# The pre norm's factor behind the FFN products: scaled on the gate, left to the post norm on the linear half

## The chip, the cores and the metric

The kernel runs on one core of one Trainium2 chip. Its metric is the time of one execution on the device in microseconds. Before the change it took 1862.63 us (median of 3 runs, 1861.44 to 1865.62).

The engines are TensorE (PE in the profile; PEld is its weight load), VectorE (DVE), ScalarE (ACT), GpSimd (POOL) and SyncE (SP), which issues the DMAs. Each engine works through its own list of instructions in the order in which it is written, and waits on semaphores.

## The reference, cut to what matters

Two transformer blocks on 272 tokens (16 meta tokens and 256 real ones) of width 1024. The first block is FFN 1, a mixer with two kinds of attention, and FFN 2. The second has a convolution, a third attention and 32 experts. The change is in the two FFNs of the first block:

```python
def rmsnorm(x, g):
    xf = x.astype(jnp.float32)
    y = xf * lax.rsqrt(jnp.mean(xf * xf, axis=-1, keepdims=True) + EPS)
    return (y * g.astype(jnp.float32)).astype(x.dtype)

def swiglu(h, w_gate, w_up, w_down):
    return (jax.nn.silu(h @ w_gate) * (h @ w_up)) @ w_down
...
        f = swiglu(rmsnorm(h, ffn1_pre_g[l]), ffn1_w_gate[l], ffn1_w_up[l], ffn1_w_down[l])
        h = h + 0.5 * rmsnorm(f, ffn1_post_g[l])
        m = hybrid_mixer(rmsnorm(h, mix_pre_g[l]), ...)
        h = h + rmsnorm(m, mix_post_g[l])
        f = swiglu(rmsnorm(h, ffn2_pre_g[l]), ffn2_w_gate[l], ffn2_w_up[l], ffn2_w_down[l])
        h = h + 0.5 * rmsnorm(f, ffn2_post_g[l])
```

Let r be the pre norm's factor of a token, rsqrt(mean + EPS). The gate product of the normed input is r times that of h times g, and so is the up product. Silu needs the factor. The up half is linear in it, and the post norm divides any factor of a token out again, but for its EPS, which has to be scaled along.

## The kernel before, in words

Tokens lie along the free dimension: 272 columns in FFN 1, 256 in FFN 2 (the meta tokens are left out there). The 1024 features are 8 tiles of 128 partitions (k = 0 to 7), and the 2816 hidden features are 22 tiles (j = 0 to 21). Every float32 product of the dense part is made of three (L676 to L678): input and weights are each split into a high part in the format fp32r and the rest, a low part.

**Weights.** They come as a stream of pieces of 128x2048 (1 MB) through a ring of 6 slots. SP issues piece p when the semaphore freed has reached p+1. ACT copies a piece into w_hi (split_piece, L1356; the copy is L1363). DVE subtracts it from the piece into w_lo (rest, L1803; L1806). There are three pairs of buffers, and ACT may overwrite one when PE has begun the piece behind its last user. An up tile j takes one piece: 8 blocks for the gate and 8 for the up half, 48 products in all.

**An FFN.** PE works through 22 up tiles into banks 2(j%2) and 2(j%2)+1, and then through 8 down tiles of 22x3 products (11 more pieces). Tile j waits for w_lo of its piece and for the hidden product of tile j-2, which frees the banks. Per tile ACT does: high part of piece j+2, Silu of the gate bank into sig (L1389). DVE does: w_lo of piece j+2, the product sig x up bank (L1886), the copy to hid_hi (L1889), the difference hid_lo (L1891), and one ada reduction (L1874; 48 tiles of another matrix, 33 in FFN 1 of which 22 lie in its up tiles, 15 in the first up tiles of FFN 2). The down products ask for hid_lo of tile k one after another.

**Ahead of an FFN.** ACT squares the residual (L1346), PE sums over partitions with a matrix of ones (L657), ACT takes the root as Ln and Exp (L1353, L1354), DVE multiplies by gain and factor into x_all (L1786), ACT copies to x_hi (L1369), DVE subtracts to x_lo (L1842). Only then does the first product of that k start. In FFN 2 the residual of the mixer (L1786, L1829) lies ahead of all this. Dummy products (L672) fill PE meanwhile.

**Behind the dense part.** SP waits for the last dense pieces and products and then loads 32 experts of 12 MB each, one behind the other (L606); each of their slots is refilled once the one ahead has been used.

## Time and profile before

| | |
|---|---|
| median of 3 runs | 1862.63 us (1861.44 to 1865.62) |
| span of the profiled execution | 1860.0 us, mean granted clock 0.991 |
| PE busy | 1788.9 us (96%) |
| DVE, ACT, POOL busy | 957.3, 524.5, 835.6 us |
| DMA | 560.93 MB, mean 302 GB/s |
| chain that ended last | PE 59%, DMA 22%, issue 5%, POOL 5%, DVE 4%, ACT 4% |
| FFN 1 | first product at 16.22, tile 1 at 24.96, up tiles until 152.4, down tiles until 218.4 us |
| FFN 2 | first product at 512.37, tile 2 at 524.21, up tiles until 638.0, down tiles until 700.3 us |

The shares of busy time are means over stages with different limits. From about 890 us on DMA is busy nearly all the time; ahead of that it is not, and PE leads the chain.

### The profile page before, as it was taken

How to read it: one execution, taken by the hardware profiler on the slowest of the kernel's cores; microseconds unless marked ns; L12 is line 12 of the kernel's file. 1: busy time of each engine (PE TensorE's matmuls, PEld its weight loads, DVE VectorE, ACT ScalarE, POOL GpSimd, SP SyncE). 2: the span in 40 equal slices, each digit the busy share in tenths (PEclk: the TensorE clock that was granted, in tenths of full speed). 3: DMA queues.
4: the chain of work that ended last, by engine and by line, in shares of the span. 5: the costliest groups of instructions: out<-in, count | busy, mean ns of one | idle time of the engine just before them, and what ended most of it. 6: DMA issues, size and time to landing. Idle time of an engine off the chain costs nothing.

```text
span 1860.0 us, 29714 instructions
## 1 busy us (share of the span) xinstructions
PE 1788.9 (96%) x10998; PEld 1127.8 (61%) x10999; DVE 957.3 (51%) x1484; ACT 524.5 (28%) x854; POOL 835.6 (45%) x487
## 2 busy tenths in 40 slices
PE   8999999998999999998999999999999999999997
PEld 7999896677899997888733333333333333333332
DVE  6776643345687574967453343344344434333334
ACT  5334453545543445446310111010010100110111
POOL 0000001000000015757277777777777767777774
PEclk9999999999999999999999999999999999999999
DMA  9777452112476552434899999999999999999995
GB/s 350 261 265 259 176 182 97 62 69 95 166 256 253 198 200 104 159 117 156 362 397 428 428 428 428 428 428 428 429 428 428 428 395 418 428 428 428 428 428 212
DMA packets 55726, 560.93 MB, mean 302 GB/s; under 512 B 6032, under 2 KB 8208, under 8 KB 14736
## 3 DMA queue, kind: packets, MB, share of 16 engines
q1 hardware_dynamic: 55520, 560.01, 74.7%
q8 instruction: 43, 0.70, 0.1%
q10 hardware_dynamic: 144, 0.07, 0.0%
q14 instruction: 19, 0.16, 0.0%
HBM read 559.00 MB, written 1.05 MB: 301 GB/s over the span
## 4 chain that ended last, share of the span: by engine, by line
PE 59%; DMA 22%; issue 5%; POOL 5%; DVE 4%; ACT 4%; POOLq 0%; SPq 0%; DVEq 0%; ACTq 0%
DMA stage<-w_exp_in 22%; PE bank L676 12%; PE bank L678 11%; PE bank L677 11%; PE bank L1216 9%; PE bank L1305 5%; POOL ring L1761 4%; PE bank L1228 1%; PE bank L1194 1%; PE bank L932 1%; PE bank L657 1%; ACT w_hi L1363 1%; DVE w_lo L1806 1%; DVE arena L1786 1%; PE bank L780 1%
## 5 line engine op out<-in xcount | busy, mean ns | idle before, releaser
L1761 POOL COPY ring<-stage 128x2048 f32<-128x2048 f32 x372 | 693.6, 1894 | 251.7 <-DMA stage<-w_exp_in 102.0
L1216 PE MATMUL bank<-ring,arena 128*64 128x512 f32 x2112 | 475.5, 597 | 15.6 <-POOL ring L1761 14.9
L676 PE MATMUL bank<-x_hi,w_hi 128*128 128x256 f32 (+1 forms) x1336 | 387.4, 290 | 8.6 <-DVE x_lo L1842 4.1
L678 PE MATMUL bank<-x_hi,w_lo 128*128 128x256 f32 (+1 forms) x1336 | 380.7, 285 | 0.0
L677 PE MATMUL bank<-x_lo,w_hi 128*128 128x256 f32 (+1 forms) x1336 | 380.4, 285 | 0.0
L1741 POOL TENSOR_TENSOR w_lo<-ring,w_hi 128x512 fp32r<-128x512 f32 x104 | 134.8, 1329 | 440.0 <-ACT w_hi L1363 440.0
L1216 PEld LDWEIGHTS bank<-ring,arena 128*64 128x64 f32 x2112 | 141.7, 136 | 313.4 <-issue 232.7
L676 PEld LDWEIGHTS bank<-x_hi,w_hi 128*128 128x128 f32 x1336 | 253.7, 190 | 22.6 <-issue 14.5
L1806 DVE TENSOR_TENSOR w_lo<-ring,w_hi 128x2048 fp32r<-128x2048 f32 x92 | 210.8, 2291 | 104.2 <-ACT w_hi L1363 102.1
L678 PEld LDWEIGHTS bank<-x_hi,w_lo 128*128 128x128 f32 x1336 | 254.0, 190 | 0.0
L677 PEld LDWEIGHTS bank<-x_lo,w_hi 128*128 128x128 f32 x1336 | 253.2, 190 | 0.4
L1363 ACT ACTIVATE w_hi<-ring 128x2048 fp32r<-128x2048 f32 x118 | 225.3, 1909 | 63.2 <-PE bank L676 63.1
L1305 PE MATMUL bank<-ring,arena 128*64 128x512 f32 x1056 | 232.2, 592 | 0.0
L2290 DVE TENSOR_SCALAR onehot<-cst 96x64 bf16<-96x64 f32 x66 | 76.5, 1159 | 235.0 <-PE bank L1228 235.0
L1708 ACT ACTIVATE cst<-cst 128x512 f32<-128x512 f32 x33 | 20.8, 630 | 511.0 <-DVE cst L1790 511.0
L1305 PEld LDWEIGHTS bank<-ring,arena 128*64 128x64 f32 x1056 | 73.9, 137 | 136.2 <-issue 127.6
L2286 DVE TENSOR_SCALAR arena<-cst,small 128x64 f32 x66 | 70.1, 1104 | 135.9 <-issue 135.9
L1731 POOL MEMSET arena<- 32x1088 f32 x1 | 1.0, 999 | 308.1 <-ACT arena L1460 308.1
L678 PE MATMUL bank<-hid_hi,w_lo 128*128 128x272 f32 (+1 forms) x352 | 100.1, 284 | 0.0
L676 PE MATMUL bank<-hid_hi,w_hi 128*128 128x272 f32 (+1 forms) x352 | 100.1, 284 | 0.0
L677 PE MATMUL bank<-hid_lo,w_hi 128*128 128x272 f32 (+1 forms) x352 | 99.8, 283 | 0.0
L1790 DVE TENSOR_SCALAR cst<-bank 128x512 f32<-128x512 f32 x33 | 22.8, 692 | 135.2 <-PE bank L1216 135.1
(352 smaller groups left out, 2058.8 us busy)
## 6 DMA issues: line engine op xcount, KB each, us to landing
stage<-w_exp_in SPq DMA_DIRECT2D x124, 2048.0 KB, 10.5
stage<-w_exp_out SPq DMA_DIRECT2D x62, 2048.0 KB, 10.6
ring<-stream SPq DMA_DIRECT2D x120, 1024.0 KB, 4.8
arena<-ada SPq DMA_DIRECT2D x48, 512.0 KB, 3.9
ring<-w_exp_in SPq DMA_DIRECT2D x8, 1024.0 KB, 8.1
ring<-w_exp_out SPq DMA_DIRECT2D x4, 1024.0 KB, 13.7
cst<-const_in SPq DMA_DIRECT2D x1, 1584.0 KB, 19.4
arena<-b_exp SPq DMA_DIRECT2D x3, 384.0 KB, 8.2
```

The lines of the kernel that those rows point to most:

```text
L676: begin = mm(out_, wh, xh, start=start, stop=False)
L677: mm(out_, wh, xl, start=False, stop=False)
L678: return begin, mm(out_, wl, xh, start=False, stop=stop)
L1216: last = mm(bank[2 + gu][pr, :], xT[:, k % 4, k // 4, :], ring[:, k, c0:c0 + 512], start=False, stop=(k == KD - 1), tile_position=pos)
L1305: last = mm(bank[5][pr, :], hmT[:, k % 4, k // 4, :], ring[:, s, c0:c0 + 512], start=False, stop=(k == KD - 1), tile_position=pos)
L1363: A(w_hi[:, BUF[p], :], ring[:, p % RING, :], ACT.Copy).then_inc(w_high, 1)
L1741: nc.gpsimd.tensor_tensor(w_lo[:, BUF[p], c:c + REST_COLS], ring[:, p % RING, c:c + REST_COLS], w_hi[:, BUF[p], c:c + REST_COLS].bitcast(f32),
L1761: nc.gpsimd.tensor_copy(ring[:, j, :], stage[:, 2 * PAIR_PLACE[j // 2 % 3] + j % 2, :]).then_inc(in_place, 1)
L1790: return V.tensor_scalar(out_, in0, s1, None, op0)
L1806: tt(w_lo[:, BUF[p], :], ring[:, p % RING, :], w_hi[:, BUF[p], :].bitcast(f32), ALU.subtract)\
L2286: last = V.tensor_scalar(S[:, t, :], slots(b_), slot[:, t, bass.ds(e_, 1)], None, ALU.is_equal)
L2290: return V.tensor_scalar(to[0:3 * E, :], const("ones", 0, SLOT_TOK, 3 * E), cst[0:3 * E, bass.ds(e_ + CONST["eye3"][0], 1)], None, ALU.mult)
```

## The change

1. **Input of the FFN.** x_hi is the residual times the gain, written by ACT (high_input), and x_lo the difference, written by DVE (lower_plain). Neither needs the factor. ACT squares the same tiles into pre_sq, POOL adds the 8 tiles into one (add_pre_squares), and PE sums them over partitions with one product (pre_sum), behind up tiles 0 and 1. The root on ACT follows that.
2. **Gate.** DVE multiplies the gate bank by the factor into sig (scale_gate), ACT applies Silu in place, DVE multiplies by the up bank.
3. **Hidden copy.** hid_hi is written by ACT in place of DVE. DVE writes hid_lo of tile j behind w_lo of the next piece.
4. **Banks.** Tile 1 uses banks 4 and 5, so tiles 1 and 2 wait for no hidden product.
5. **Post norm.** Its EPS is multiplied by mean + EPS of the pre norm: one operation of DVE in tile 0 writes EPS times the sum of squares, and one more product on PE adds it to the sum; ACT adds EPS squared.
6. **First loads.** The input is laid out by partition and loaded in two halves; the first piece comes in two halves, of which the gate half is first; the first gains come by ACT's queue. DVE's two halvings of gains go behind piece 1.
7. **FFN 2's start.** DVE's lower_plain lies between the operations of the mixer's residual, and ACT splits piece 2 there in quarters.

The diff, cut to its core:

```diff
@@ PE @@
+                def pre_sum():
+
+                    pe.wait_ge(pre_added, AT[pre_added][n] + KD - 1)
+                    mm(bank[7][:, 0:w], const("ones"), sq_sum[:, 0:w], start=True, stop=True).then_inc(n_sum, 1)
...
+                else:
+                    for j in range(2):
+                        up_tile(j, ORDER[at] + j + 1, None, first=(j == 0))
+                pre_sum()
+                for j in range(2, ahead):
+                    up_tile(j, ORDER[at] + j + 1, hidden_before(j))
...
-            norm_sum("f1_pre", KD, TOK)
-            keep_running(10)
+            keep_running(16)
             ffn(0, FFN1_AT, 0)
-            norm_sum_of_two("f1_post", TOK)
+            norm_sum_of_two("f1_post", TOK, scaled_eps=rtmp)
...
-            norm_sum("f2_pre", KD, SEQ)
-            keep_running(10)
             ffn(1, FFN2_AT, META)
@@ ACT @@
+                for j in range(NF):
+                    if f == 0 or j:
+                        split_piece(at + j + 2)
+                    act.wait_ge(gate_scaled, base + j + 1)
+                    A(sig[:, j % 2, 0:w], sig[:, j % 2, 0:w], ACT.Silu).then_inc(exp_ready, 1)
+                    act.wait_ge(hid_ready, base + j + 1)
+                    A(hid_hi[:, j, 0:w], hid[:, 0:w], ACT.Copy).then_inc(hid_high, 1)
...
+            split_piece(FFN1_AT + 1)
+            for m in range(KD):
+                square_input(m, res[:, m, :])
             act.wait_ge(const_sem, 16)
             root("f1_pre", TOK, D, "eps1")
-            split_input("f1_pre", x_all, TOK)
-            split_piece(FFN1_AT + 1)
...
-            squares("f2_pre", KD, lambda m: real(res[:, m, :]), updated["m1"])
+            for m in range(KD):
+                act.wait_ge(updated["m1"], m + 1)
+                high_input("f2_pre", m, real(res[:, m, :]), META)
+                square_input(m, real(res[:, m, :]))
+                if 2 <= m < 6:
+                    split_piece(FFN2_AT + 2, m - 2, 4)
             root("f2_pre", SEQ, D, "eps1")
@@ POOL @@
+                    nc.gpsimd.tensor_tensor(s, s, pre_sq[:, m - 1, 0:width], ALU.add).then_inc(pre_added, 1)
@@ DVE @@
+                def scale_gate(j):
+
+                    if j == 0:
+                        dve.wait_ge(n_rs, AT[n_rs][pre] + 1)
+                    dve.wait_ge(up_ready, base + j + 1)
+                    tt(sig[:, j % 2, 0:w], bank[up_bank(j)][:, 0:w], rstd[:, 0:w], ALU.mult).then_inc(gate_scaled, 1)
+                    if j == 0:
+                        ts(rtmp[:, 0:w], sq_sum[:, 0:w], EPS1, None, ALU.mult)
...
                 for j in range(NF):
                     if at + j + 2 in DVE_PIECES:
                         rest(at + j + 2)
-                    hidden(j)
+                    if j:
+                        lower_hidden(j - 1)
+                    scale_gate(j)
+                    if j == 0:
+                        dve.wait_ge(c_silu, f + 1)
                     if f == 0:
                         ada_tile(j)
                     elif ADA_FIRST + j < ADA_TILES:
                         ada_tile(ADA_FIRST + j)
+                    hidden(j)
+                lower_hidden(NF - 1)
```

**ACT inside FFN 1.** These are three up tiles of the part of before that is written out without a loop. L1363 writes w_hi, L1389 is the Silu:

```order
L1363 ACTIVATE w_hi<-ring 128x2048 [waits freed,slot_in2]
L1389 ACTIVATE arena<-bank 128x272 [waits up_ready]
L1363 ACTIVATE w_hi<-ring 128x2048 [waits freed,slot_in3]
L1389 ACTIVATE arena<-bank 128x272 [waits up_ready]
L1363 ACTIVATE w_hi<-ring 128x2048 [waits freed,slot_in4]
L1389 ACTIVATE arena<-bank 128x272 [waits up_ready]
```

And the first tiles of after (L1406 writes w_hi, L1433 is the Silu, L1435 the copy to hid_hi):

```order
L1406 ACTIVATE w_hi<-ring 128x2048 [waits freed,slot_in3]
L1433 ACTIVATE arena<-arena 128x272 [waits gate_scaled]
L1435 ACTIVATE hid_hi<-arena 128x272 [waits hid_ready]
L1406 ACTIVATE w_hi<-ring 128x2048 [waits freed,slot_in4]
L1433 ACTIVATE arena<-arena 128x272 [waits gate_scaled]
L1435 ACTIVATE hid_hi<-arena 128x272 [waits hid_ready]
```

Between the Silu of a tile and the next piece there stands now a copy that waits for DVE's product (hid_ready), and the Silu waits for DVE's scaling (gate_scaled) in place of PE's tile.

**DVE inside FFN 1,** one tile before (w_lo, product, hid_hi, hid_lo, and ada as two rows):

```order
L1806 TENSOR_TENSOR w_lo<-ring,w_hi 128x2048 [waits w_high]
L1886 TENSOR_TENSOR arena<-arena,bank 128x272 [waits hid_split,exp_ready]
L1889 CAST hid_hi<-arena 128x272 [waits hid_ready]
L1891 TENSOR_TENSOR hid_lo<-arena,hid_hi 128x272 [waits hid_high]
L1874 ISA arena,small<-arena 128x1024 [waits ada_used,ada_in1]
L1874 ISA small 128x1
L1806 TENSOR_TENSOR w_lo<-ring,w_hi 128x2048 [waits w_high]
```

And after (w_lo, hid_lo of the tile ahead, scaling, ada as two rows, product):

```order
L1874 TENSOR_TENSOR w_lo<-ring,w_hi 128x2048 [waits w_high]
L1987 TENSOR_TENSOR hid_lo<-arena,hid_hi 128x272 [waits hid_high]
L1973 TENSOR_TENSOR arena<-bank,rstd 128x272 [waits up_ready]
L1959 ISA arena,small<-arena 128x1024 [waits ada_used,ada_in0]
L1959 ISA small 128x1
L1982 TENSOR_TENSOR arena<-arena,bank 128x272 [waits hid_split,exp_ready]
L1874 TENSOR_TENSOR w_lo<-ring,w_hi 128x2048 [waits w_high]
```

The scaling and the product now stand behind w_lo of the next piece but one, and hid_lo is one tile late.

**ACT at the start of FFN 1,** before (L1353 and L1354 the root, L1369 x_hi, L1363 pieces 1 and 2, L1421 the Silu of c):

```order
L1353 ACTIVATE rtmp<-bank,cst 128x272 [waits norm_sum,const_in]
L1354 ACTIVATE rstd<-rtmp 128x272 [waits act_chain]
L1369 ACTIVATE x_hi<-arena 128x272 [waits normed] x8
L1363 ACTIVATE w_hi<-ring 128x2048 [waits slot_in1]
L1339 ACT_TABLE_LOAD
L1421 ACTIVATE arena<-arena 128x1024 [waits c_in]
L1395 UNCONDITIONAL_BRANCH
L1395 ISA
L1363 ACTIVATE w_hi<-ring 128x2048 [waits slot_in2]
```

And after (L1406 piece 1, L1453 squares, L1395 and L1396 the root, L1474 the Silu of c, then piece 2):

```order
L1406 ACTIVATE w_hi<-ring 128x2048 [waits slot_in1]
L1453 ACTIVATE arena<-res 128x272 x8
L1395 ACTIVATE rtmp<-bank,cst 128x272 [waits norm_sum,const_in]
L1396 ACTIVATE rstd<-rtmp 128x272 [waits act_chain]
L1381 ACT_TABLE_LOAD
L1474 ACTIVATE arena<-arena 128x1024 [waits c_in]
L1406 ACTIVATE w_hi<-ring 128x2048 [waits slot_in2]
L1433 ACTIVATE arena<-arena 128x272 [waits gate_scaled]
```

The root, which waits for the sum behind up tile 1, stands ahead of piece 2, which up tile 2 needs. Before, the root stood ahead of piece 1 and of all products.

## Rows read from the trace of the kernel before

**Rows 1.** The page of the profile, part 4: shares of the chain that ended last, by line.

```profile
DMA stage<-w_exp_in 22%; PE bank L676 12%; PE bank L678 11%; PE bank L677 11%; PE bank L1216 9%; PE bank L1305 5%; POOL ring L1761 4%; PE bank L1228 1%; PE bank L1194 1%; PE bank L932 1%; PE bank L657 1%; ACT w_hi L1363 1%; DVE w_lo L1806 1%; DVE arena L1786 1%; PE bank L780 1%
```

**Rows 2.** Windows: stretch, its length, busy us and instructions of PE, PEld, DVE, ACT, POOL; granted clock, DMA share, GB/s.

```profile
20.70:152.40 131.70, 131.68 (x1040) 131.30 (x1041) 99.94 (x129) 52.38 (x48) 0.00 (x0) 1.00 0.76 278
524.20:638.00 113.80, 113.79 (x962) 113.80 (x963) 87.14 (x113) 44.98 (x41) 0.00 (x0) 1.00 0.71 254
460.00:470.00 10.00, 7.73 (x65) 7.39 (x64) 8.16 (x13) 2.96 (x4) 0.00 (x0) 1.00 0.28 105
226.00:228.00 2.00, 2.00 (x6) 1.36 (x6) 1.65 (x5) 1.33 (x4) 0.00 (x0) 0.50 0.00 0
1000.00:1860.00 860.00, 830.36 (x4134) 296.28 (x4130) 341.56 (x500) 89.57 (x162) 636.33 (x342) 1.00 0.98 414
```

**Rows 3.** Timeline of DVE, one tile of FFN 1 (start us, us, engine, line, operation, idle before).

```profile
86.22 0.44 DVE L1886 TENSOR_TENSOR arena<-arena,bank 128x272 f32<-128x272 f32 x1 [1.45 <-ACT arena L1389]
86.69 0.30 DVE L1889 CAST hid_hi<-arena 128x272 fp32r<-128x272 f32 x1
87.03 0.44 DVE L1891 TENSOR_TENSOR hid_lo<-arena,hid_hi 128x272 fp32r<-128x272 f32 x1
87.39 1.22 DVE L1874 CUSTOM_DVE_ANT_0 arena<-arena 128x1024 f32<-128x1024 f32 x1
...
88.53 2.29 DVE L1806 TENSOR_TENSOR w_lo<-ring,w_hi 128x2048 fp32r<-128x2048 f32 x1
92.28 0.44 DVE L1886 TENSOR_TENSOR arena<-arena,bank 128x272 f32<-128x272 f32 x1 [1.46 <-ACT arena L1389]
```

**Rows 4.** Timeline of ACT, the same tile of FFN 1.

```profile
85.79 0.40 ACT L1389 ACTIVATE arena<-bank 128x272 f32<-128x272 f32 x1 [3.85 <-PE bank L678]
86.09 1.91 ACT L1363 ACTIVATE w_hi<-ring 128x2048 fp32r<-128x2048 f32 x1
```

**Rows 5.** Groups of 0 to 420 us, shapes apart (count, busy us, mean ns, idle before).

```profile
L1369 ACT ACTIVATE x_hi<-arena 128x272 fp32r<-128x272 f32 x16 | 6.7, 428 | 6.2 <-DVE arena L1786 6.2
```

**Rows 6.** Timeline of all engines, start of FFN 1.

```profile
6.51 2.67 ACT L1346 ACTIVATE sq<-res 128x272 f32<-128x272 f32 x8 [3.98 <-DMA res<-xT_in]
...
12.63 0.49 ACT L1353 ACTIVATE rtmp<-bank,cst 128x272 f32<-128x272 f32 x1 [0.23 <-PE bank L657]
13.15 0.43 ACT L1354 ACTIVATE rstd<-rtmp 128x272 f32<-128x272 f32 x1
...
22.60 1.28 ACT L1339 ACT_TABLE_LOAD   x1
...
23.89 1.06 ACT L1421 ACTIVATE arena<-arena 128x1024 f32<-128x1024 f32 x1
...
24.96 0.39 PE L676 MATMUL bank<-x_hi,w_hi 128*128 128x272 f32 x1
```

**Rows 7.** Tile ring, 0 to 20 us: landing of the first pieces.

```profile
DMA to landing us min/median/max: 7.7/13.6/21.4
```

**Rows 8.** Timeline of DVE, from mix_post's root to FFN 2.

```profile
502.53 0.88 DVE L1786 SCALAR_TENSOR_TENSOR arena<-arena,col,rstd 128x256 f32<-128x256 f32 x2 [3.49 <-ACT rstd L1354]
503.33 0.42 DVE L1829 TENSOR_TENSOR res<-res,arena 128x256 f32<-128x256 f32 x1
```

**Rows 9.** Timeline of PE, first products and third tile of FFN 2.

```profile
512.37 0.36 PE L676 MATMUL bank<-x_hi,w_hi 128*128 128x256 f32 x1 [0.37 <-DVE x_lo L1842]
...
524.21 0.35 PE L676 MATMUL bank<-x_hi,w_hi 128*128 128x256 f32 x1 [0.31 <-DVE arena L1886]
```

**Rows 10.** Timeline of ACT, two late tiles of FFN 2.

```profile
609.64 0.39 ACT L1389 ACTIVATE arena<-bank 128x256 f32<-128x256 f32 x1 [3.49 <-PE bank L678]
...
615.33 0.38 ACT L1389 ACTIVATE arena<-bank 128x256 f32<-128x256 f32 x1 [3.49 <-PE bank L678]
```

**Rows 11.** Timeline of PE, a wait in the output products before FFN 2.

```profile
469.54 0.36 PE L676 MATMUL bank<-y_sb_hi,w_hi 128*128 128x256 f32 x1 [1.14 <-DVE w_lo L1806]
```

**Rows 12.** The page, part 5: POOL's subtraction.

```profile
L1741 POOL TENSOR_TENSOR w_lo<-ring,w_hi 128x512 fp32r<-128x512 f32 x104 | 134.8, 1329 | 440.0 <-ACT w_hi L1363 440.0
```

More of the change, by code:

```diff
@@ L416, in build @@
         FIN_ORDER = (0, 1, 4, 5, 2, 3, 6, 7)
-        x_in = sem("x_in")
+        x_in = [sem(f"x_in{i}") for i in range(2)]
+        w_first_in = sem("first_half_piece_in")
+        w_first_high = sem("first_half_piece_high")
+        w_first_lower = sem("first_half_piece_lower")
+        gain_sem = sem("first_gain_in")
+        pre_added = sem("pre_squares_added")
+        gate_scaled = sem("gate_scaled")
         const_sem = sem("const_in")
@@ L694, in first_tiles @@
                                 c0 = (g * KD + k) * P
-                                begin, last = three(bank[2 * j + g][:, 0:w], w_hi[:, j, c0:c0 + P],
+                                begin, last = three(bank[up_bank(j) + g][:, 0:w], w_hi[:, j, c0:c0 + P],
                                                     w_lo[:, j, c0:c0 + P], x_hi[:, k, lo:TOK], x_lo[:, k, lo:TOK],
@@ L703, in up_tile @@
                 def up_tile(j, piece, hid_at, first=False):
-                    pe.wait_ge(w_lower, piece)
-                    pe.wait_ge(hid_ready, hid_at)
+                    if first:
+                        pe.wait_ge(w_first_lower, 1)
+                    else:
+                        pe.wait_ge(w_lower, piece)
+                    if hid_at is not None:
+                        pe.wait_ge(hid_ready, hid_at)
                     for g in range(2):
+                        if first and g:
+                            pe.wait_ge(w_lower, piece)
                         for k in range(KD):
@@ L1383, in ffn @@
                 base = f * NF
-                def step(j, ready, it=None, split=True):
-                    if split:
-                        split_piece(at + j + 2, it)
-                    act.wait_ge(up_ready, ready)
-                    A(sig[:, j % 2, 0:w], bank[(j % 2) * 2][:, 0:w], ACT.Silu).then_inc(exp_ready, 1)
-                whole = NF // RING
-                if f:
-                    for j in range(RING):
-                        step(j, base + j + 1, split=(j > 0))
-                with act.Fori(f, whole) as it:
-                    for j in range(RING):
-                        step(j, it * RING + (base + j + 1), it)
-                for j in range(whole * RING, NF):
-                    step(j, base + j + 1)
+                for j in range(NF):
[5 more added lines that the diff above has]
+                    A(hid_hi[:, j, 0:w], hid[:, 0:w], ACT.Copy).then_inc(hid_high, 1)
                 m = 0
@@ L1820, in normed, with residual @@
                 then(tiles - 1)
-            def residual(n, src, gain, into, upd):
+            def residual(n, src, gain, into, upd, behind=lambda m: None):
                 dve.wait_ge(n_rs, AT[n_rs][n] + 1)
@@ L1862, in _ @@
             added = {}
-            rest(FFN1_AT)
-            normed("f1_pre", KD, lambda m: res[:, m, :], lambda m: vec("f1_pre", m), lambda m: x_all[:, m, :],
-                   lower("f1_pre", x_all, TOK))
+            half = PIECE // 2
+            dve.wait_ge(w_first_high, 1)
+            tt(w_lo[:, 0, 0:half], ring[:, 0, 0:half], w_hi[:, 0, 0:half].bitcast(f32), ALU.subtract)\
+                .then_inc(w_first_lower, 1)
+            dve.wait_ge(gain_sem, 16)
+            for m in range(KD):
+                lower_plain("f1_pre", m, res[:, m, :], 0)
+                if m == 5:
+                    dve.wait_ge(w_high, ORDER[FFN1_AT] + 1)
+                    tt(w_lo[:, 0, half:], ring[:, 0, half:], w_hi[:, 0, half:].bitcast(f32), ALU.subtract)\
+                        .then_inc(w_lower, 1)
             rest(FFN1_AT + 1)
-            dve.wait_ge(c_silu, 1)
+            dve.wait_ge(cols_sem, 16)
+            mark(ts(half_f1, vec("f1_post", 0, 8), 0.5, None, ALU.mult))
+            mark(ts(half_f2, vec("f2_post", 0, 8), 0.5, None, ALU.mult))
             def ada_tile(n):
```

141 lines of the change are left out of this document (92 added, 49 removed).

## The prediction

> **What bounds the kernel now.** I read the page's chain first, then the windows, then the timelines of DVE and ACT inside one FFN tile, then the two places where an FFN starts. The chain ends in the loads of the expert weights [rows 1], and from 1000 to 1860 us DMA is at 0.98 [rows 2]. But SP issues these loads only behind waits on the last dense pieces and products, in which the three product lines of TensorE lead the chain. So every microsecond that the dense part wins or loses moves the end by as much. In both FFNs the up products are bound by TensorE: it is busy for 131.68 of 131.70 us and 113.79 of 113.80 us [rows 2]. A tile (48 products) takes 6.06 us in FFN 1 (86.22 to 92.28, [rows 3]) and 5.69 in FFN 2 [rows 10]. DVE and ACT run beside it with slack: before each tile's product DVE sat idle for 1.45 us, and ACT for 3.85 us before its Silu [rows 3, 4].
>
> **What makes that slack.** Before, ACT goes from the Silu of tile j straight to the high part of weight piece j+3 (85.79, then 86.09, [rows 4]), while DVE does its three hidden operations and the ada reduction. The two engines meet once in a tile. I write a step on DVE from start to start: 0.36 us for an element-wise operation of 272 columns (87.03 to 87.39), 1.14 for ada (87.39 to 88.53); an instruction starts 0.08 before the one ahead of it ends. The Silu ends at 86.19 and DVE starts at 86.22, so a handoff is 0.03; the next ACT instruction starts 0.10 before the Silu ends [rows 3, 4].
>
> **The change in the loop of tiles.** The cast to hid_hi (0.30 on DVE) goes to ACT, where a copy of this shape takes 0.43 [rows 3, 5]; a scaling of the gate out of PSUM is added on DVE, which I price as the product that reads the same bank, 0.44 [rows 3]. Busy time is nearly unchanged: DVE 0.36 + 1.14 + 0.44 + 2.21 + 0.36 = 4.5 us per tile, ACT 2.7. By busy time both fit under 6.06. What counts is the order. ACT's list is now: piece j+3, Silu, copy of hid_hi, next piece; and the copy waits for DVE's product. DVE's list is: w_lo of piece j+3, hid_lo of tile j, scaling of tile j+1, ada, product. So the work closes into a ring, in which each link waits for the one ahead:
>
> scaling 0.36, ada 1.14, product 0.44, handoff 0.03, copy 0.43 - 0.10, high part 1.91, handoff 0.03, w_lo 2.29 - 0.08, hid_lo 0.36: sum 6.81 us [rows 3 to 5]. (The Silu, 0.40, lies beside ada.)
>
> 6.81 is more than 6.06, so the ring sets the step and TensorE waits about 0.75 us ahead of each tile, on w_lo. With 256 columns the same sum is 6.75; the operations are 0.02 shorter (0.42 for 0.44, [rows 8]). From tile 15 of FFN 2 there is no ada left (48 tiles, 33 of them done in FFN 1): the product then starts behind the Silu, at 0.42 + 0.03 + 0.42 + 0.03 = 0.90 instead of 0.34 + 1.14 = 1.48, and the step is 6.17, still over 5.69.
>
> **FFN 1, start.** The squares, their sum and the root go away from ahead of the first product. But the root now stands on ACT ahead of piece 2. Landings: x (1.1 MB) landed by 6.5 [rows 6], and the smallest landing time of a piece, 7.7 us [rows 7], fits piece 0 issued right behind it: about 9.0, so some 2.4 us per MB. The new order puts 3.5 MB up to the end of piece 1: estimate 6.5 + 2.4 x 2.4 = 12.3. High part 1.91, w_lo 2.29: tile 1 starts at 16.5 instead of 24.96 and ends at 22.6. Then in series: sum of squares 0.5 (23.1; three products of this kind take 2.00 us at a granted clock of 0.50, six instructions in [rows 2], so one is 0.33 to 0.67), Ln 0.52, Exp 0.45, table load 1.28, Silu of c 0.97 to the next start, piece 2's high part 1.91, its w_lo 2.29 [rows 3, 4, 6]: 30.6. Before, tile 2 started at 24.96 + 6.06 = 31.0. So 8 us of head start shrink to 0.4. Bounds: with landings as early as 9 us the start is 27.5 (-3.5); with POOL's seven additions at the 1.33 us that its 128x512 subtraction takes [rows 12] instead of the 0.71 in proportion that I take, they end at 23.9, which gives 31.9 (+0.9).
>
> **FFN 1, sum.** Let W be the start of tile 2. Tile 3 waits for w_lo of piece 3, one ring behind W less the hid_lo and with one extra small operation: W + 6.7. Then 19 steps of 6.81 up to the down products: W + 136.1, against 31.0 to 152.4, that is 121.4: +14.7. The last hid_lo comes 7.09 + 2.87 = 9.96 us behind that, and the down products ask for it after 21 x 0.379 = 7.96: +2.0. The rest of the down products keeps its pace. FFN 1: 14.7 + 2.0 - 0.4 = +16.3 us.
>
> **FFN 2, start.** DVE's residual (0.40, then 0.33, [rows 8]) gets x_lo in between: 1.13 us per k, under the 1.42 that TensorE needs for its 12 products. The first x_lo is done at 502.53 + 0.40 x 2 + 0.33 + 0.40 + 0.48 = 504.5, so the products start at 504.6 instead of 512.37 [rows 9], and tile 2 at 504.6 + 11.4 + 0.5 = 516.6 instead of 524.21. POOL's additions lie behind those products (last square about 513, one addition 0.7 to 1.3). Then the root: 516.6 + 0.52 + 0.43 + 1.29 + 0.97, but the Silu of c must end before ada: 519.9. Ada 1.14, product 0.42, copy 0.36, high part 1.91, w_lo 2.29 with handoffs: 526.1. Tile 3 would have started at 524.2 + 5.69 = 529.9 before. So 3.8 us are kept of 7.8.
>
> **FFN 2, sum.** From 526.1: 14 steps of 6.75 and 5 of 6.17 give 125.4: the down products start at 651.5 against 638.0 [rows 2]: +13.5. The last hid_lo comes 6.43 + 2.22 = 8.65 behind, asked for after 21 x 0.356 = 7.5: +1.2. FFN 2: +14.7 us, its start included.
>
> **Total.** 16.3 + 14.7 = +31.0. The profiled span of 1860.0 becomes 1891; the median of the runs is 1862.6, 2.6 above the span, and becomes 1893.6. The extra product of the post norm waits for nothing new (its input is ready since tile 0) and lies ahead of the last squares; cost 0, at most 0.6 twice.
>
> **The clock.** While TensorE is fed thinly its granted clock has been 0.50, that is 1.2 GHz (226 to 228 us, [rows 2]). In the new start TensorE stands for 7.5 us from 23.1, so tile 2 may run at 1.2 GHz and take up to 12.1. That costs nothing: tile 4 is only due at W + 13.5 and the ring leaves 0.75 per tile to catch up. Would the waits of 0.75 in every 6.81 us pull the clock down? Between 460 and 470 TensorE is busy for 7.73 of 10 us, with a wait of 1.14 in it, at 1.00 [rows 2, 11]. The Trainium skill ("TensorE: Matmul & The Clock Gate", A second HAM failure mode: psum-queue depth-cycling) says that small idles between groups of matmuls can be frequent enough for the clock to swing between its two levels. By that rule the tiles would take up to 12.1 us each; this is rival 4.
>
> **Rivals.**
> 1. *The ring is shorter than TensorE's tile* (faster). It decides below 6.06 in FFN 1 and 5.69 in FFN 2. Then only the starts count: -0.4 + 0.6 and -3.8: 1859. For it: busy sums of 4.5 and 2.7 us. Against: it needs 0.75 off a sum whose links have rows in their own shape, and three quarters of it are two of them (1.91 and 2.29). 4%.
> 2. *A shorter ring that still binds*, 0.25 over the tile on average: 38 x 0.25 + 2.2 for the last hid_lo, less 3.6 for the starts: +8, 1871. 5%.
> 3. *A longer ring*: the scaling and the product that read PSUM, or waits on two semaphores, take 0.3 more: 38 x 0.3 = +11, 1905. 7%.
> 4. *The clock falls inside the loop*: a tile at 1.2 GHz takes 12.1, 5.3 over the ring; eight such tiles give +42, 1935. 2%.
> 5. *Forecast*, with its own bounds (start -3.5 to +0.9, ring within 0.15 us): 1885 to 1900. 82%.
>
> **Numbers.** Predicted 1894. The range 1884 to 1903 leaves out rivals 1, 2, 4 and part of 3. A change below 0.2% (3.7 us) can't be told from none; rival 1 counts as faster with nearly all its 4%, rival 2 reaches into no change with 1 to 2%: faster 4%, same 2%, slower 94%.
>
> **What would show it.** In the changed profile: DVE's scalings 6.8 us apart in FFN 1; TensorE idle before the first product of each tile, 0.7 to 0.8 us, released by w_lo; ACT's high parts starting behind the hid_hi copy; a gap of TensorE from about 23 to 30.6; in FFN 2 steps of 6.75, then 6.17; FFN 2's first product 2.1 us behind the start of the residual, where it was 9.8 (502.53 to 512.37). Wrong would be: tiles 6.06 apart (rival 1), w_lo starting before the product of the same tile, or a granted clock under 1 in the loop.

## The result and the profile after

The changed kernel takes 1901.76 us (median of 4 runs, 1899.09 to 1906.11) against 1864.12 for the kernel before beside it: ratio 1.0202, 95% interval [1.0185, 1.0219]. Forecast were 1894 and 1884 to 1903. The profiled execution spans 1900.3 us (before 1860.0), at a mean granted clock of 0.986 (0.991).

I cut the execution at four roots of the norms (the Ln on ACT). Each column is the time from the root ahead of it (the first from the start) to its own, from the one profiled execution of each kernel; the last column is the median of all its runs, in us:

```
                                 to root of   to root of   to root of   to root of   median
                                 f1_post      mix_post     f2_post      final        of runs
                                 (FFN 1)      (mixer 1)    (FFN 2)      (rest)
before                           220.5        281.1        200.7        1150.2       1864.1
after                            239.3        277.6        218.7        1157.0       1901.8
order (Silu, piece, copy)        223.1        279.3        200.5        1153.6       1866.2
copy on DVE                      225.1        277.7        200.4        1156.3       1867.4
ada last                         227.6        278.9        209.9        1148.7       1875.8
piece 2 before the root          235.2        280.5        218.6        1157.5       1900.4
2 products for 16                237.6        277.5        218.8        1153.2       1901.5
FFN 2's squares on DVE           239.7        277.7        217.2        1152.8       1896.2
order + piece 2                  219.1        279.5        200.5        1154.8       1863.1
all together                     219.5        280.5        198.9        1156.7       1863.4
starts moved up                  220.3        277.4        202.2        1154.0       1864.9
the same, 16 products            220.4        279.4        201.9        1157.2       1865.7
starts mended                    215.3        277.4        198.9        1156.3       1857.9
```

The change costs +18.9 in FFN 1 and +18.0 in FFN 2. The stretches between and behind them are all but untouched by the edit, and move too: -3.5 and +6.9. The part on the prediction comes back to them. Where an experiment names the kernel before, the ratio is to its runs beside that experiment, with medians of 1863.9 to 1865.0.

The ring in FFN 1, on DVE (timeline of the changed kernel: start us, us, engine, line, operation; the columns of [rows 3]):

```profile
91.90 2.29 DVE L1874 TENSOR_TENSOR w_lo<-ring,w_hi 128x2048 fp32r<-128x2048 f32 x1 [2.30 <-ACT w_hi L1406]
94.11 0.43 DVE L1987 TENSOR_TENSOR hid_lo<-arena,hid_hi 128x272 fp32r<-128x272 f32 x1
94.46 0.43 DVE L1973 TENSOR_TENSOR arena<-bank,rstd 128x272 f32<-128x272 f32 x1
94.81 1.22 DVE L1959 CUSTOM_DVE_ANT_0 arena<-arena 128x1024 f32<-128x1024 f32 x1
...
95.95 0.43 DVE L1982 TENSOR_TENSOR arena<-arena,bank 128x272 f32<-128x272 f32 x1
98.69 2.29 DVE L1874 TENSOR_TENSOR w_lo<-ring,w_hi 128x2048 fp32r<-128x2048 f32 x1 [2.30 <-ACT w_hi L1406]
```

And on ACT, the same tile:

```profile
94.93 0.43 ACT L1433 ACTIVATE arena<-arena 128x272 f32<-128x272 f32 x1 [3.06 <-DVE arena L1973]
96.42 0.43 ACT L1435 ACTIVATE hid_hi<-arena 128x272 fp32r<-128x272 f32 x1 [1.05 <-DVE arena L1982]
96.76 1.90 ACT L1406 ACTIVATE w_hi<-ring 128x2048 fp32r<-128x2048 f32 x1
```

Read them together: product at 95.95, copy at 96.42, high part at 96.76, w_lo at 98.69. The copy waits for the product, the high part is queued behind the copy, w_lo waits for the high part, and the next product is queued behind w_lo. A step is 98.69 - 91.90 = 6.79 us, where before it was 6.06 [rows 3]. DVE stood for 1.45 us in each tile before and now stands for 2.30, though it has no more work than before (about 4.6 us in a tile, now 4.5). What this does to TensorE, from a window of the changed kernel (length, PE busy, clock, DMA share, GB/s) and from the page's group of the first of its three product lines:

```profile
60.00:170.00 110.00, 102.06 (x781) 1.00 0.63 232
```

```profile
L701 PE MATMUL bank<-x_hi,w_hi 128*128 128x256 f32 (+1 forms) x1336 | 395.0, 296 | 40.3 <-DVE arena L1982 20.0
```

It is busy for 102.06 of 110 us at full clock, where before the up tiles showed 131.68 of 131.70 [rows 2]. TensorE itself, at the start of two tiles:

```profile
89.66 0.39 PE L701 MATMUL bank<-x_hi,w_hi 128*128 128x272 f32 x1 [0.40 <-DVE arena L1982]
96.44 0.39 PE L701 MATMUL bank<-x_hi,w_hi 128*128 128x272 f32 x1 [0.47 <-DVE arena L1982]
```

It is released by the product at 95.95, which frees the bank of two tiles ago, and not by w_lo, done at 94.19. The ring is the same; TensorE hangs on another of its links than I wrote, 2.2 us later in the step.

The start of FFN 1 in the changed kernel, TensorE (timeline):

```profile
7.06 6.12 PE L697 MATMUL bank<-cst 128*128 128x128 f32 x32 [7.06 <-DMA cst<-const_in]
...
25.11 0.62 PE L714 MATMUL bank<-arena,cst 128*128 128x272 f32 x2
33.33 0.59 PE L701 MATMUL bank<-x_hi,w_hi 128*128 128x272 f32 x1 [7.59 <-DVE w_lo L1874]
```

and ACT between the last two:

```profile
25.83 0.49 ACT L1395 ACTIVATE rtmp<-bank,cst 128x272 f32<-128x272 f32 x1 [8.51 <-PE bank L714]
26.35 0.43 ACT L1396 ACTIVATE rstd<-rtmp 128x272 f32<-128x272 f32 x1
26.80 1.28 ACT L1381 ACT_TABLE_LOAD   x1
28.09 1.06 ACT L1474 ACTIVATE arena<-arena 128x1024 f32<-128x1024 f32 x1
29.05 1.89 ACT L1406 ACTIVATE w_hi<-ring 128x2048 fp32r<-128x2048 f32 x1
```

The keep-running products of L697 wait for the constants (landed at 7.06) and end at 13.18; the first real product comes at 12.93. Then the chain sum, root, table, Silu of c, high part, w_lo leaves TensorE idle for 7.59 us, and the granted clock falls to 0.50:

```profile
30.00:38.00 8.00, 4.67 (x20) 4.67 (x21) 4.72 (x7) 3.61 (x4) 0.00 (x0) 0.50 0.48 179
```

The start of FFN 2, DVE and then POOL of the changed kernel (timelines):

```profile
520.10 0.42 DVE L1894 TENSOR_TENSOR res<-res,arena 128x256 f32<-128x256 f32 x1
...
521.49 0.96 DVE L1894 TENSOR_TENSOR res<-res,arena 128x256 f32<-128x256 f32 x1
...
523.03 0.48 DVE L1855 SCALAR_TENSOR_TENSOR x_lo<-res,col,x_hi 128x256 fp32r<-128x256 f32 x1 [0.18 <-ACT x_hi L1449]
523.43 0.96 DVE L1894 TENSOR_TENSOR res<-res,arena 128x256 f32<-128x256 f32 x1
...
533.14 2.82 DVE L1874 TENSOR_TENSOR w_lo<-ring,w_hi 128x2048 fp32r<-128x2048 f32 x1
```

```profile
521.44 0.73 POOL L1795 TENSOR_TENSOR arena<-arena 128x256 f32<-128x256 f32 x1 [184.00 <-ACT arena L1453]
...
533.09 0.73 POOL L1795 TENSOR_TENSOR arena<-arena 128x256 f32<-128x256 f32 x1 [1.21 <-ACT arena L1453]
```

The residual's addition (L1894) takes 0.42 until POOL's first addition has begun 0.05 ahead of one; from there it takes 0.96, and a step of the residual 1.94 where the one ahead of it took 1.39 (520.10 to 521.49). The w_lo behind the last addition takes 2.82 instead of 2.29.

### The profile page after: what moved, and what is told of

Its sections match the earlier page's. It is cut to its first block, busy times and chain, and to the rows that moved or that the text cites. A ratio compares the mean times of both kernels' runs of the same rounds, so it can differ in the third digit from the quotient of the medians.

```text
span 1900.3 us, 29659 instructions
## 1 busy us (share of the span) xinstructions
PE 1796.5 (95%) x10966; PEld 1131.8 (60%) x10967; DVE 951.8 (50%) x1471; ACT 543.5 (29%) x901; POOL 847.6 (45%) x501
## 4 chain that ended last, share of the span: by engine, by line
PE 45%; DMA 22%; issue 10%; DVE 9%; ACT 8%; POOL 4%; POOLq 0%; SPq 0%; DVEq 0%; ACTq 0%
DMA stage<-w_exp_in 22%; PE bank L1257 9%; PE bank L701 7%; PE bank L703 7%; PE bank L702 7%; ACT w_hi L1406 5%; PE bank L1346 5%; POOL ring L1830 4%; DVE arena L1959 2%; DVE w_lo L1874 2%; PE bank L1269 2%; PE bank L1235 2%; PE bank L975 1%; DVE hid_lo L1987 1%; DVE arena L1982 1%
## 5 line engine op out<-in xcount | busy, mean ns | idle before, releaser
L1830 POOL COPY ring<-stage 128x2048 f32<-128x2048 f32 x372 | 693.5, 1894 | 254.2 <-DMA stage<-w_exp_in 98.4
L701 PE MATMUL bank<-x_hi,w_hi 128*128 128x256 f32 (+1 forms) x1336 | 395.0, 296 | 40.3 <-DVE arena L1982 20.0
L701 PEld LDWEIGHTS bank<-x_hi,w_hi 128*128 128x128 f32 x1336 | 257.9, 193 | 61.3 <-issue 22.5
L702 PEld LDWEIGHTS bank<-x_lo,w_hi 128*128 128x128 f32 x1336 | 258.0, 193 | 0.4
L703 PEld LDWEIGHTS bank<-x_hi,w_lo 128*128 128x128 f32 x1336 | 258.1, 193 | 0.0
L1406 ACT ACTIVATE w_hi<-ring 128x2048 fp32r<-128x2048 f32 (+1 forms) x120 | 223.3, 1862 | 52.5 <-PE bank L701 51.1
L2386 DVE TENSOR_SCALAR arena<-cst,small 128x64 f32 x66 | 76.4, 1200 | 135.8 <-issue 135.8
L1795 POOL TENSOR_TENSOR arena<-arena 128x272 f32<-128x272 f32 (+1 forms) x14 | 12.0, 855 | 207.1 <-ACT arena L1453 206.2
```

The source lines that it names most:

```text
L701: begin = mm(out_, wh, xh, start=start, stop=False)
L702: mm(out_, wh, xl, start=False, stop=False)
L703: return begin, mm(out_, wl, xh, start=False, stop=stop)
L1406: last = A(w_hi[:, BUF[p], part * n:part * n + n], ring[:, p % RING, part * n:part * n + n], ACT.Copy)
L1830: nc.gpsimd.tensor_copy(ring[:, j, :], stage[:, 2 * PAIR_PLACE[j // 2 % 3] + j % 2, :]).then_inc(in_place, 1)
L2386: last = V.tensor_scalar(S[:, t, :], slots(b_), slot[:, t, bass.ds(e_, 1)], None, ALU.is_equal)
```

## Experiments

All start from the changed kernel, and each has its row in the table above.

**The order on ACT.**

```diff
-                for j in range(NF):
-                    if f == 0 or j:
-                        split_piece(at + j + 2)
+                if f == 0:
+                    split_piece(at + 2)
+                for j in range(NF):
                     act.wait_ge(gate_scaled, base + j + 1)
                     A(sig..., ACT.Silu).then_inc(exp_ready, 1)
+                    if j + 1 < NF:
+                        split_piece(at + j + 3)
                     act.wait_ge(hid_ready, base + j + 1)
```

> ScalarE's order alone: Silu(j), then the high part of piece j + 3, then the high part of hidden(j); before the loop of FFN 1 the high part of piece 2. Theory (the ring of scaling, ada, product, copy, high part, lower part holds every up tile): the high part now starts behind the Silu (0.33) instead of behind ada and product (1.14 + 0.44) and copy (0.33), so the ring is 0.36 + 0.03 + 0.33 + 1.90 + 0.03 + 2.21 + 0.36 = 5.2 us, under TensorE's tile (6.06 at 272 columns, 5.69 at 256). TensorE's waits ahead of the tiles (20.0 us in 36) go, each FFN gives 15 to 17 us back, less 3 for the tile at 1.2 GHz that is no longer hidden: 1868 to 1875 us, the step in both loops 6.05 and 5.69. Rival (the time is in VectorE's added busy time or in TensorE's clock, and the order does not matter): 1895 to 1902, the waits only change their names.

Measured 1866.24, ratio to before 1.0011 [0.9999, 1.0022], 2 us better than the range. Nothing was taken off any engine; 35.5 us came back. In its timeline of ACT the high part follows the Silu at once:

```profile
88.96 0.43 ACT L1433 ACTIVATE arena<-arena 128x272 f32<-128x272 f32 x1 [3.50 <-DVE arena L1975]
89.30 1.90 ACT L1406 ACTIVATE w_hi<-ring 128x2048 fp32r<-128x2048 f32 x1
91.11 0.41 ACT L1437 ACTIVATE hid_hi<-arena 128x272 fp32r<-128x272 f32 x1
```

and DVE now waits for TensorE:

```profile
88.48 0.44 DVE L1975 TENSOR_TENSOR arena<-bank,rstd 128x272 f32<-128x272 f32 x1 [0.67 <-PE bank L703]
...
94.54 0.44 DVE L1975 TENSOR_TENSOR arena<-bank,rstd 128x272 f32<-128x272 f32 x1 [0.66 <-PE bank L703]
```

6.06 from tile to tile: TensorE's own step. The ring is the cause of the loss in the loops: in FFN 1 every step from the seventh on is 6.05 to 6.06, in FFN 2 the later ones are 5.68. The rival (busy work or clock) falls.

**The copy back on DVE.** ACT's two copy lines of the loop go, and DVE gets, behind its product:

```diff
+                    dve.wait_ge(hid_ready, n)
+                    V.tensor_copy(hid_hi[:, j, 0:w], hid[:, 0:w]).then_inc(hid_high, 1)
```

> The high part of hidden alone goes back to VectorE, as in the kernel before; ScalarE does Silu and the piece only, still in that order. Theory: what makes the ring long is that ScalarE's high part of the piece is queued behind the copy, which waits for VectorE's product. Without the copy in its queue it starts behind the Silu: ring 0.36 + 0.03 + 0.33 + 1.90 + 0.03 + 2.21 + 0.36 (hid_lo) = 5.2, VectorE's own busy sum 2.21 + 0.36 + 0.36 + 1.14 + 0.44 + 0.26 = 4.8, both under the tile: 1868 to 1876. Rival 1 (ada between scaling and product is what costs): no change, 1900. Rival 2 (VectorE is the bound by its busy time): slower than e1 by about 0.26 x 38 = 10 us, 1880 to 1886.

Measured 1867.36, 1.0014 [1.0004, 1.0024]. Two quite different edits that both free the high part from the product give the same time: it is the queue behind the copy, not the copy's length. Rival 1 (no change, 1900) falls, and rival 2 (DVE's busy time) is 13 us off at its nearest.

**Ada behind the product.** In DVE's loop `hidden(j)` stands ahead of the two branches of `ada_tile`.

> VectorE's order alone: the product of sig and up ahead of the ada tile instead of behind it. Theory: the ring loses ada (1.14) and gets the Silu's own time and two handoffs (0.33 + 0.06) instead, and then ends at the later of ada and copy plus high part; 0.36 + 0.39 + 0.44 + 0.03 + 0.33 + 1.91 + 0.03 + 2.21 + 0.36 = 6.1 in all tiles, against 6.79 and 6.71 with ada now. FFN 1 (19 tiles, TensorE's 6.06): 12 us back; FFN 2 (13 tiles with ada, 6.71 to 6.06): 8 us back: 1880 to 1885. Rival (the order on ScalarE alone sets it and ada is hidden): no change, 1898 to 1903.

Measured 1875.77, 1.0072 [1.0053, 1.0091]: 26 us back, more than the 17 to 22 expected.

```profile
39.54 0.43 DVE L1973 TENSOR_TENSOR arena<-bank,rstd 128x272 f32<-128x272 f32 x1
...
45.77 0.43 DVE L1973 TENSOR_TENSOR arena<-bank,rstd 128x272 f32<-128x272 f32 x1
```

The ring is 6.23 here in FFN 1, not 6.1 (6.15 in FFN 2), and the two FFNs got back 11.7 and 8.8 us (table), 20.5 together and as expected. The other 5 lie outside (mixer 1 +1.3, the rest -8.4, and how the profiled run lies to the median), where no code differs. So this run shows that ada's place is one link of the ring; what came back beyond that is taken up below, under the unchanged stretches.

**Piece 2 ahead of FFN 1's root.** `split_piece(FFN1_AT + 2)` behind the squares, no split at j = 0 of FFN 1's loop.

> Start of FFN 1 alone: the high part of piece 2 ahead of the first root instead of behind the root, the table load and the Silu of c. Theory: tile 2 waits 7.6 us (25.7 to 33.33) for the chain of squares' sums, root, table load, Silu of c, high part, lower part. Piece 2 has landed at 21.4, so its lower part is done at 25.6; tile 2 starts at 25.7. Tile 3 then waits for root, ada, product, copy, high and lower part of piece 3: about 35.2 instead of 40.0, 4.8 us earlier; the loop's step stays 6.79: 1896 to 1898. Rival (the start is hidden or given back by a tile at 1.2 GHz): within 1 us of 1901.

Measured 1900.39, 1.0196 [1.0178, 1.0214]: the number that the rival gave, not mine. FFN 1 ended 4.2 us earlier, near the 4.8 expected, but mixer 1 took 2.9 more and the whole is not told apart from the changed kernel. The start is real in its place. In mixer 1 the clock stood at 0.50 for 20.5 us in this run and for 13.7 in the changed kernel's, which at half the pace is worth 3.4: what was won at the start was lost to the clock in mixer 1, not inside the FFN.

**Two keep-running products instead of 16.** `keep_running(16)` becomes `keep_running(2)`.

> The 16 products that only keep TensorE running ahead of FFN 1's first tile become 2. Theory: tile 0 starts at 12.93 because the constants land at 7.06 and 16 products of 0.38 us follow them, not because of piece 1; with 2 it starts at about 8, and tile 1, held by its lower part (15.0 to 17.1), at 17.1 instead of 19.2, tile 2 about 2 us earlier than 33.3: 1899 to 1900. Rival (the products keep the clock up, and without them tiles 0 and 1 run at 1.2 GHz, 5 to 9 us longer): 1902 to 1908.

Measured 1901.46, 1.0207 [1.0187, 1.0226]: between the two ranges, and not told apart from the changed kernel. TensorE in its timeline:

```profile
6.97 1.22 PE L697 MATMUL bank<-cst 128*128 128x128 f32 x4 [6.97 <-DMA cst<-const_in]
...
8.49 0.43 PE L702 MATMUL bank<-x_lo,w_hi 128*128 128x272 f32 x1
8.72 0.43 PE L703 MATMUL bank<-x_hi,w_lo 128*128 128x272 f32 x1
...
17.09 0.39 PE L701 MATMUL bank<-x_hi,w_hi 128*128 128x272 f32 x1 [0.75 <-DVE w_lo L1874]
23.24 0.67 PE L714 MATMUL bank<-arena,cst 128*128 128x272 f32 x2
31.51 0.60 PE L701 MATMUL bank<-x_hi,w_hi 128*128 128x272 f32 x1 [7.60 <-DVE w_lo L1874]
```

Tile 1 starts at 17.09 as computed, and tile 2 1.8 us earlier. So the 16 products did hold the first tile. They also kept it fast: until about 10.9 us its products start 0.23 apart here (8.49, 8.72), where the changed kernel's start 0.12 to 0.13 apart from the first on (13.14, 13.26). The rival's slow pace is real, then, but it lasted for some 12 products, and tile 0 had that time to spare, since tile 1 waits for its w_lo until 17.09 anyway. FFN 1 is 1.7 shorter.

**FFN 2's squares added on DVE.** POOL's second `add_pre_squares` goes; DVE adds square m - 1 ahead of x_lo of chunk m.

```diff
+            def square_and_lower(m):
+                if m > 1:
+                    add_pre_square(m - 1)
+                lower_plain("f2_pre", m, real(res[:, m, :]), META)
```

> FFN 2 alone: the seven additions of squares go from GpSimd to VectorE, each between two steps of the residual; the rest as in the changed kernel. Theory: an addition on VectorE takes 0.96 instead of 0.42 while one of GpSimd's runs beside it, so that a step of the residual takes 1.94 instead of 1.40; with the additions on VectorE (0.34 each) a step is 0.40 + 0.34 + 0.40 + 0.34 = 1.5, the last lower part of the input at 12.5 instead of 15.3 us behind the first root, and tile 3 up to 3 us earlier: 1898 to 1900. Rival (the 0.96 is a property of the addition behind ScalarE's read of the same residual, not of GpSimd): the additions stay at 0.96, a step becomes 2.3, and tile 3 comes 3 us later: 1904 to 1906.

Measured 1896.20, 1.0173 [1.0153, 1.0193].

```profile
523.40 0.42 DVE L1893 TENSOR_TENSOR res<-res,arena 128x256 f32<-128x256 f32 x1
523.73 0.48 DVE L1854 SCALAR_TENSOR_TENSOR arena<-arena,col,rstd 128x256 f32<-128x256 f32 x1
524.13 0.42 DVE L1918 TENSOR_TENSOR arena<-arena 128x256 f32<-128x256 f32 x1
524.46 0.48 DVE L1854 SCALAR_TENSOR_TENSOR x_lo<-res,col,x_hi 128x256 fp32r<-128x256 f32 x1
524.86 0.42 DVE L1893 TENSOR_TENSOR res<-res,arena 128x256 f32<-128x256 f32 x1
```

With nothing on POOL, every addition takes 0.42 again and a step 1.46, although DVE has more to do. The rival falls: the 0.96 was POOL's. FFN 2 got 1.5 us of it, where I expected up to 3; the median moved by 5.6, beyond the range and again more than the stretch that was edited.

**Order and piece 2.** Both edits.

> ScalarE's order (Silu, high part of piece j + 3, high part of hidden) together with the high part of piece 2 ahead of the first root. Theory: apart, the second brought 4.2 us at the end of FFN 1. With a ring of 5.3 us, tile 3 waits for root, table, Silu of c, high and lower part of piece 3 only, until about 33.7, and TensorE then never waits: end of FFN 1 at 218 to 219 instead of 223.1, the whole at 1860 to 1863. Rival (what is won there is lost behind, as it was in the run with piece 2 alone, where 4.2 us at the end of FFN 1 left 0.8 at the end): end of FFN 1 at 218 to 219, the whole at 1864 to 1867.

Measured 1863.05, 0.9993 [0.9982, 1.0005]: as expected, at the edge of both ranges. FFN 1 ended at 219.1, 4.1 under the order alone; the whole is 3.2 under it. The rival's "lost behind" is not borne out as a rule. Tile 3 still waited 1.89 us (until 34.16), so "never waits" was wrong.

**All together.** Those two, POOL's second additions on DVE, FFN 2's piece 3 split ahead of its root, and FFN 1's sum product between the halves of tile 1.

> All together: ScalarE's order of the ring, piece 2 ahead of the first root, the product of ones and summed squares between the two halves of tile 1 (root at 23 instead of 25.8), the additions of FFN 2's squares on VectorE, and FFN 2's piece 3 split ahead of its root. Theory (FFN starts and ring were all that the change lost; what it removes, normed input and its wait, is then gained): FFN 1 ends 3 to 5 us ahead of before (216 to 218), FFN 2 takes 196 to 198 from the root of mix_post to that of f2_post instead of 200.7: 1853 to 1859. Rival (the up tiles are bound by TensorE from their first tile, so that an earlier start gains only what the first tiles waited, and the rest is lost to tiles at 1.2 GHz): 1862 to 1866.

Measured 1863.43, 0.9993 [0.9978, 1.0007]: a miss, 4 us over my range and inside the rival's. FFN 1 ended at 219.5, not at 216 to 218: the sum product stood at the right place but waited for POOL's additions, so the root came at 25.92 as ever and TensorE waited 2.79 us in the middle of tile 1. FFN 2 came to 198.9, 1 to 3 over what I expected.

**Starts moved up.** Pieces 2 and 3 ahead of both roots, 4 behind Silu(0), 5 behind Silu(1), none behind Silu(2); all additions of squares on DVE; 2 products. And the same with 16.

> On ScalarE's order of the ring: pieces 2 and 3 split ahead of each FFN's root, piece 4 behind Silu(0), 5 behind Silu(1), none behind Silu(2); the additions of squares of both FFNs on VectorE; FFN 1's product of ones and sum between the halves of tile 1; 2 products instead of 16 ahead of the first tile. Theory (each start was held by what these move): in FFN 1 tile 2 starts at 23 to 24 instead of 31.0 before the change and no tile behind it waits, so its end is at 212 to 214 instead of 220.46; FFN 2 takes 196 to 198 instead of 200.7 from root to root: 1852 to 1857, about 0.5% faster than before the change. Rival (gains at the starts are given back behind, as in the two combined runs): the ends of the FFNs come earlier as said, but the whole is at 1860 to 1864.

> The run before with the 16 products kept. Theory: tile 0 starts at 12.9 and not at 8, tile 1 at 19.2 instead of 17.1: 2 us later at the end of FFN 1, 1854 to 1859. Rival (the products keep the clock up, without them the first tiles are at 1.2 GHz): not later, or up to 5 us earlier.

Measured 1864.94, 1.0006 [0.9995, 1.0018], and 1865.73, 1.0012 [0.9999, 1.0025]. Both expectations missed, by 8 and 7 us, and the first one's rival too: FFN 1 ended at 220.3 and 220.4. In the first of them TensorE:

```profile
41.57 0.59 PE L701 MATMUL bank<-x_hi,w_hi 128*128 128x272 f32 x1 [4.99 <-DVE arena L1995]
```

and ACT ahead of it:

```profile
21.96 1.92 ACT L1409 ACTIVATE w_hi<-ring 128x2048 fp32r<-128x2048 f32 x1 [2.88 <-DMA ring<-stream]
...
29.78 1.92 ACT L1409 ACTIVATE w_hi<-ring 128x2048 fp32r<-128x2048 f32 x1 [2.38 <-DMA ring<-stream]
```

Pieces 3 and 4 were not there yet (21.9, 29.7). In one queue, work asked for too early is as bad as work too late: ACT stood for a landing, and the root, or the copy of hidden(0), stood behind it. With the start bound by landings the 2 or 16 products made no difference (0.1 at the end of FFN 1).

FFN 2 came to 202.2 and 201.9, 3 us over all together, and there no landing is waited for. TensorE stands for product 2 ahead of tile 4, in all together and then in the first of these:

```profile
530.67 0.45 PE L701 MATMUL bank<-x_hi,w_hi 128*128 128x256 f32 x1 [1.94 <-DVE arena L2000]
```

```profile
530.66 0.58 PE L701 MATMUL bank<-x_hi,w_hi 128*128 128x256 f32 x1 [4.27 <-DVE arena L1995]
```

The difference of 2.3 us, most of the 3, is one w_lo (2.29): with the pieces moved up, DVE subtracts piece 4 ahead of scaling 1 and piece 5 ahead of scaling 2, so that one more subtraction stands ahead of product 2. The same order holds in FFN 1. Too early is a matter of DVE's queue too, and not of landings alone.

**Starts mended.** All together, with FFN 1's additions on DVE too, 2 products, and only piece 2 ahead of FFN 1's root.

> As the run with all together, with FFN 1's additions of squares on VectorE too and 2 products instead of 16 ahead of its first tile; in FFN 1 only piece 2 is split ahead of the root, since piece 4 lands at 29.7 and VectorE stood still for it in the last two runs. Theory: root of FFN 1 at 20.7 to 22, tile 2 at 23.3, tile 3 at about 31.3 (34.2 in the run with order and piece 2), tile 4 at 38.3 (40.2): end of FFN 1 at 217 to 217.5; FFN 2 root to root 199: 1859 to 1861 as a whole. Rival (the stretches behind the FFNs move by more than is won here, with TensorE's clock): end of FFN 1 as said, the whole anywhere from 1861 to 1866.

Measured 1857.92 (10 runs, 1855.71 to 1862.10), 0.9969 [0.9956, 0.9981] against the kernel before: 0.3% faster than before, and 2.3% faster than the changed kernel; 1 us better than the range. TensorE's waits from its first tile to 60 us:

```profile
17.30 0.39 PE L701 MATMUL bank<-x_hi,w_hi 128*128 128x272 f32 x1 [0.76 <-DVE w_lo L1868]
20.93 0.73 PE L714 MATMUL bank<-arena,cst 128*128 128x272 f32 x2 [0.35 <-DVE arena L1913]
37.91 0.39 PE L701 MATMUL bank<-x_hi,w_hi 128*128 128x272 f32 x1 [1.12 <-DVE arena L1992]
```

Root at 21.76 and tile 4 at 37.91, as computed (38.3); no wait of tile 2 or 3 is left. FFN 1 is 5.2 us and FFN 2 1.8 us shorter than before the change. So with the ring opened, its additions off POOL and its starts mended, the change is worth some 6 us. That holds for the change with all that came with it (loads, banks and these edits): how much of the 6 us the norm's move alone brings, no run separates.

## Why the prediction was right, and where it was off

**The ring: right, and shown.** Summed 6.81, measured 6.79; 6.75 against 6.72 in FFN 2 with ada, 6.17 against 6.16 without. The order of ACT's operations was as forecast. (The two long links, 1.91 and 2.29, are 62% of the sum, not the three quarters that rival 1 says.) Two edits that open the ring return 34 to 36 us, and one that shortens it to 6.23 returns a part.

**What TensorE hangs on: wrong, and made good by luck.** Its waits are released by the product, where I wrote w_lo: 0.40 to 0.57 us in FFN 1 where I wrote 0.7 to 0.8, and in FFN 2 0.78 to 0.82 with ada and 0.21 to 0.26 without. The step does not depend on this, but the sum does, once for each FFN: tile 4 started 15.61 us behind tile 2 (33.33, 48.94) where I had 13.5, and in FFN 2 8.86 behind tile 3 (544.97, 553.83) where I had 6.75. Each time I had 2.1 too little. Against that, the last up tile takes TensorE's own time and not a step of the ring, 0.7 less in FFN 1, and the down products' waits for the last hid_lo, put at 2.0 and 1.2, came as 0.27 and none. So each FFN's sum is nearer than its terms were.

**FFN 1's start: a term was mis-sized.** W (tile 2) was put at 30.6 (27.5 to 31.9); it was 33.33. I bounded tile 1 by the landing of piece 1 and left the keep-running products out. The constants land at 7.06 (3.6 before; another load now stands ahead of theirs on ACT's queue, and more is loaded beside them, but with the same loads they landed at 5.4 in the run with ACT's order, so the landing itself varies). 16 products follow, and tile 0 starts at 12.93, so that the sum product comes at 25.11 instead of 22.6. The chain behind it took 8.22 against 8.0. With 2 products, tile 1 started at 17.09 (I had 16.5). W lay 1.4 outside my own bounds. FFN 1: +18.9 against +16.3. The 2.7 of W is the whole difference only because the terms of the paragraph above nearly cancel: the down products started 18.3 us later than before (152.2, 170.53) where I had 14.3, and behind their start 0.5 us was lost where I had 2.0.

**FFN 2's start: a term was mis-sized, twice.** I had 24.0 us from the first root's Exp (502.08) to tile 3; it was 27.5 (517.45 to 544.97). A step of the residual was put at 1.13, hidden under TensorE's 1.42. It is 1.40 even without POOL (x_lo stands for x_hi, 0.18 idle and the 0.08 by which DVE's instructions else overlap), which would still be hidden, and 1.94 with it. Taking POOL away brings tile 3 to 25.9: 1.6 us. Most of what is left is TensorE's clock: it stood for 2 us ahead of the first product, and in the kernel with POOL's additions away the windows read

```profile
521.00:524.50 3.50, 3.50 (x19) 0.52 0.57 206
524.50:534.00 9.50, 9.50 (x83) 1.00 0.09 36
```

These are 19 products in 3.5 us at 0.52, that is 1.2 GHz for nearly all of it, where full speed (83 in 9.5) puts 30: 1.3 us. I had such a slow stretch in FFN 1 (it came, 0.50 from 30 to 38 us, and was absorbed as forecast), not here, where first products bind. FFN 2: +18.0 against +14.7, tile 3 being 3.5 of it.

The contention between DVE and POOL I had not priced at all: I placed POOL's additions behind TensorE's products and did not ask whom they run beside. The Trainium skill (SBUF — State Buffer, Who interferes with whom) says that a DVE instruction with two inputs in SBUF contends with a GpSimd instruction that reads SBUF, that what they share is held as an exclusive lock, and that the order of issue decides who waits. The trace agrees on who waits: POOL's 0.73 began 0.05 ahead (521.44 to 522.17), and the addition came out 0.54 longer, ending 0.28 behind POOL's. A wait for POOL's end with the whole 0.42 behind it would have been 0.68, so a part of the addition's 0.42 is not held up.

**The unchanged stretches.** -3.5 in mixer 1 and +6.9 behind FFN 2, together +3.4, were forecast as nothing. Over the thirteen kernels these two spread over 3.7 and 8.8 us. Short falls of the granted clock to 0.50, of 3.4, 6.8 or 10.2 us, come at other places in each kernel. The clearest case is the stretch from the root of ln_var to that of n2, in the second block, in windows of the kernel before and then of the changed one:

```profile
839.78:904.60 64.82, 59.32 (x483) 1.00 0.56 210
```

```profile
874.10:942.45 68.35, 62.38 (x483) 0.95 0.53 199
```

The same 483 products take 3.5 us longer. Over all thirteen profiled executions this stretch takes 64.8 to 68.4 us, and 64.5 to 65.1 when half of the time at 0.50 is taken off; the stretch ahead of it, from n1's root to ln_var's, 127.2 to 130.3, and 126.8 to 127.3. So here the clock is the cause. In mixer 1 the time at 0.50 is 23.9 us before and 13.7 after, worth 5.1, of which 3.5 shows. Behind FFN 2 it is 6.8 and 13.6, worth 3.4 of the 6.9; 2.4 more lie in the experts, from n2's root to final's (947.9 and 950.3, at 1.00 in all thirteen, spread 4.4), and their cause stays open. With ada last and with FFN 2's squares on DVE the profiled execution had no fall in the stretch from n1 to ln_var, and none or one of 3.4 us in the next, where the changed kernel's had 6.8 in each: 6.6 and 4.5 us, about what those two medians moved by beyond the stretches that were edited. What makes a fall come or not stays open.

**The total.** +37.6 us in the medians, where I had +31; the two FFNs make up 36.9 of it. 1901.76 lies inside the range but over the 1900 that I gave the forecast's own bounds (item 5 of the rivals): the starts of both FFNs were mis-sized by more than these allowed.

**Rivals.** 1 and 2 (a ring under or just over the tile) fell by the 6.79, 4 (clock falling in the loop) by the 1.00 between 60 and 170 us in spite of a wait in every tile. Rival 3's total (1905) is near the result, but for another reason: the links were 0.02 shorter, not 0.3 longer.

## What to carry to other kernels

Busy time per tile (4.5 and 2.7 us under 6.06) did not show the loss here, since two engines hand work back and forth: follow the chain through both queues until it closes, and ask of each in-order queue what stands behind a waiting instruction. Putting the long, ready work (here 1.9 us of weight split) between two short dependent ones, instead of behind them, was worth 35 us with the same instructions. Work can also be asked for too early: a split ahead of its landing blocks ACT's queue as a late operand does, and a subtraction moved ahead of a scaling delays all that hangs on the scaling by its own 2.3 us.
